# Retention's rotary halves crossed by ScalarE while it evacuates a block, and top-k rounds moved behind the rotations

## The chip, the cores and the metric

The kernel runs on one core of one Trainium2 chip. The metric is the device time of one execution in microseconds (us); the time before is the median of 3 runs. Engines are called PE (TensorE, the matmuls), DVE (VectorE), ACT (ScalarE), POOL (GpSimd) and SP (SyncE, which issues DMAs).

## The reference

One inference step of a two-layer decoder trunk for 256 prompt tokens and 8 x 8 sample tokens, 320 tokens in all. What matters here is the first layer's mixer (`even_mixer`), in fp32:

```python
proj = h @ p['w_in_even'][e]
q, k, v, qi, wi, ki, rq, rk, rv, rg = jnp.split(proj, points, axis=-1)
...
rq = rope(rq.reshape(B, L, RET_HEADS, RET_HEAD_DIM), pos, inv_r)
rk = rope(rk.reshape(B, L, RET_HEADS, RET_HEAD_DIM) * (RET_HEAD_DIM ** -0.5), pos, inv_r)
...
def rope(x, pos, inv_freq):      # half = 64 of a head's 128 for retention, 8 of 64 for the attention
    x1, x2 = xf[..., :half], xf[..., half:rot]
    return concat([x1 * cos - x2 * sin, x2 * cos + x1 * sin, xf[..., rot:]])
```

The other head group picks keys by `lax.top_k` of an indexer's score (64 of 256 prompt keys, 66 of 264 keys for the samples).

## The kernel before

Every engine has its own instruction stream, written out by hand; semaphores order them. Features lie on the 128 partitions, the 320 tokens along a row. The input projection of the mixer (stage `even_in`) gives 26 blocks of 128 output features. A block is 8 contraction chunks of 3 matmuls (`three_passes`, lines 1610 to 1612: the weight's high part times the activation's high and low part, and the weight's low part times the high one), each 128x320. Two blocks share a weight tile (`w_raw`, 1 MB, two slots). Before PE may use a tile, ACT rounds it to `w_hi` (line 1880, two instructions) and DVE subtracts to get `w_lo` (line 2073, two instructions); SP loads the tile after next into `w_raw` once `w_lo` is done. ACT evacuates a finished block from one of four PSUM banks to `proj` (line 857) and signals `p_evac`.

Blocks 0 to 7 hold the attention's and indexer's queries and keys, 10 to 17 the retention's queries and keys (`B_RQK` = 10), 18 to 25 its values and gates. Blocks 0 to 7 and 10 to 17 are rotated in place:

```python
pe.matmul(ps[:, 4 + r % 2, 0:TOK], perm[:, kind, :], proj[:, b, :], ...)            # L589, the halves swapped and signed
dve.tensor_tensor(rope_a[:, par, :], src, ropet[:, 2 * kind, :], ALU.mult)          # L965, times cos
steps.did(dve.tensor_tensor(rope_b[:, par, :], ps[:, 4 + par, 0:TOK], ...))         # L967, times sin, waits rope_mm
dve.tensor_tensor(src, rope_a[:, par, :], rope_b[:, par, :], ALU.add)               # L970
```

The program names `rope_a` and `rope_b` as `f`, whose memory they use. PE issues the permutation product of block b-1 behind all of block b's matmuls, and small products of the indexer behind some blocks (`after(b)`). DVE goes round once for every two blocks b, b+1 (`dve_even`): `w_lo` of the next tile, then the two rotations, then what the step has besides: index scores, and rounds of the top-k (`top`: MAX of 8, MATCH_REPLACE; lines 975 and 977), which overwrite the 8 largest scores of each row; `mask` (lines 983 and 985) turns what was taken into a bias. `scores[0]` is 128 wide (first 128 queries), `scores[1]` 256, `score_s` 326. All of this must be done before the attention, which begins with `logits(0)` on PE, a MEMSET (line 1142) and `soft(0)` on DVE, after the last block's evacuation. The rest of `score_s`'s rounds stand in the attention. In the attention PE multiplies with the retention state `st_in` (line 735), which POOL loads after the last evacuation, and streams weights of the conditioning (line 1675).

Of the kernel before, what the change touches and what calls it, by code (L numbers as in the profile page):

```python
# [23 lines left out]
P = 128  # L24
# [3 lines left out]
ALU = mybir.AluOpType  # L28
# [9 lines left out]
TOK = PTOK + STOK  # L38
# [14 lines left out]
HD = 64  # L53
# [19 lines left out]
B_RQK = 10  # L73
# [73 lines left out]
CR = 2  # L147
# [41 lines left out]
def build(nc, t):  # L189

    with ExitStack() as ctx:
        sems = {}

        def sem(name):
            if name not in sems:
                sems[name] = ctx.enter_context(nc.semaphore(name))
            return sems[name]
# [65 lines left out]
        ps = ctx.enter_context(nc.psum_tensor("ps", [P, 8, 512], F32))  # L263
# [15 lines left out]
        stack, pb = phase()  # L279
# [6 lines left out]
        stack, pb = phase()  # L286
# [4 lines left out]
        stack.close()  # L291
        stack, pb = phase()
        proj = pb("proj", [P, EVEN_BLOCKS, TOK])
        perm = pb("perm", [P, 2, P])
        cached = pb("cached", [P, NB, 3, PAST])

        bias_p = pb("bias_p", [P, 2, PTOK])
# [154 lines left out]


        p_evac = sem("p_evac")
        rope_mm = sem("rope_mm")
        rope_done = sem("rope_done")
        perm_in, rope_in = sem("perm_in"), sem("rope_in")
        even_in_dma, even_const = sem("even_in_dma"), sem("even_const")
# [104 lines left out]
        def even_constants(sp_):  # L563

            sp_.wait_ge(w_used, CR + W_BASE["even_in"])
            sp_.wait_ge(moments_done, SUB["down0"] + 1)
            sp_.dma_start(perm[:, :, :], t["perm"]).then_inc(perm_in, 16)
# [14 lines left out]
        def pe_even(pe, three_passes, w_half, two_tiles, ada_pieces, ada_transpose):  # L582
            base = W_BASE["even_in"]

            def rotate(b, r, kind):

                pe.wait_ge(p_evac, PB + b + 1)
                pe.wait_ge(rope_done, CR + r - 1)
                pe.matmul(ps[:, 4 + r % 2, 0:TOK], perm[:, kind, :], proj[:, b, :], start=True, stop=True)\  # L589
                  .then_inc(rope_mm, 1)  # L590

            def block_of(n, b, bank, slot_, h):
# [77 lines left out]

            two_tiles("even_in", True)
            pe.wait_ge(row_ready, 6)
            rotate(0, 0, 0)
            rotate(1, 1, 0)
            for b in range(4, EVEN_BLOCKS):
                block_of(base + b // 2, b, b % 4, (base + b // 2) % 2, b % 2)
                if b <= 9:
                    rotate(b - 2, b - 2, 0)
                elif B_RQK < b <= B_RQK + 8:
                    rotate(b - 1, b - 1 - (B_RQK - 8), 1)  # L680
                after(b)


# [161 lines left out]
        def act_even(act, steps, split_w, n_half, ada_copy):  # L845
            base = W_BASE["even_in"]

            def evacuate(t_, j, b, kinds):

                if t_:  # L850
                    split_w(base + t_ + 1, (base + j + 1) % 2)
                for h in range(2):
                    if h == 0:
                        act.wait_ge(half_used, t_ + 1)
                    else:
                        act.wait_ge(w_used, CR + base + t_ + 1)
                    act.activation(proj[:, b + h, :], ps[:, 2 * j + h, 0:TOK], kinds[h][0], scale=kinds[h][1])\
                       .then_inc(p_evac, 1)

# [98 lines left out]
        def dve_even(dve, steps, split_w, softplus, ada_bias):  # L958
            base = W_BASE["even_in"]

            def rotate(b, r, par, kind):

                dve.wait_ge(p_evac, PB + b + 1)
                src = proj[:, b, :]
                dve.tensor_tensor(rope_a[:, par, :], src, ropet[:, 2 * kind, :], ALU.mult)  # L965
                dve.wait_ge(rope_mm, r + 1)
                steps.did(dve.tensor_tensor(rope_b[:, par, :], ps[:, 4 + par, 0:TOK], ropet[:, 2 * kind + 1, :],  # L967
                                            ALU.mult))
                steps.wait()
# [33 lines left out]
            for b in range(0, EVEN_BLOCKS, 2):  # L1003
# [28 lines left out]
                    dve.reduce_sum(wis1[:, :], wis[:, :, :], axis=AX).then_inc(wis_ready, 1)  # L1032
                    score(0, 0, range(NIH))
                if B_RQK <= b < B_RQK + 8:
                    rotate(b, b - B_RQK + 8, 0, 1)
                    rotate(b + 1, b - B_RQK + 9, 1, 1)
                if b == 12:
                    top(scores[0], 3)
                elif b == 14:
                    score(1, 1, (0, 1))  # L1040
                    score(1, 2, (2, 3))
                    top(scores[0], 2)
                elif b == 16:
                    top(scores[0], 3)
                    mask(scores[0], bias_p[:, 0, 0:P])
                elif b == 18:
                    dve.wait_ge(wis_ready, 1)
                    for bh in range(2):
                        dve.wait_ge(relu_ready, 4 + bh)
                        last = dve.tensor_scalar(relu[:, 1 - bh, 0:KEYS_S], relu[:, 1 - bh, 0:KEYS_S],  # L1050
                                                 wis1[:, bh:bh + 1], None, ALU.mult)
                    last.then_inc(weighed, 1)
                    top(scores[1], 3)
                elif b == 20:
                    top(scores[1], 3)
                elif b == 22:
                    top(scores[1], 2)
                    mask(scores[1], bias_p[:, 1, :])
                    dve.wait_ge(ixs_done, 1)
                    steps.did(dve.tensor_tensor(score_s[:, 0:KEYS_S], ps[0:STOK, 6, 0:KEYS_S], bias_s[:, :], ALU.add))  # L1060
                    steps.wait()
                    top(score_s[:, :], 2)
                elif b == 24:
                    top(score_s[:, :], 1)

            def spread(h):
                dve.wait_ge(tr_v, h + 1)
# [1381 lines left out]
def tables():  # L2449
# [7 lines left out]
    perm = np.zeros((P, 2, P))  # L2457
# [4 lines left out]
    for kind, starts, half, inv in ((0, (0, HD), 8, inv_a), (1, (0,), 64, inv_r)):  # L2462
        ang = pos[None, :] * inv.astype(np.float32)[:, None]
        for s in starts:
            for i in range(half):
                perm[s + half + i, kind, s + i] = -1.0
                perm[s + i, kind, s + half + i] = 1.0
            for o in (s, s + half):
                rope[o:o + half, 2 * kind] = np.cos(ang)
                rope[o:o + half, 2 * kind + 1] = np.sin(ang)  # L2470
    out["perm"], out["rope"] = perm, rope

    lg = np.array(LN_G)
# [124 lines left out]
```

## Time and profile before

| | us |
|---|---|
| median of 3 runs | 1431.97 (1431.39, 1431.97, 1434.85) |
| profiled execution, own time | 1434.27 |
| its span | 1431.4 |
| PE busy | 1362.2 |
| DVE busy | 790.0 |
| ACT busy | 613.5 |

Times within the trace count from the span's start. `even_in` runs from about 320 to 428 us; block 10 begins at about 355 us, block 12 at 366.04, block 18 at 396.07, block 22 at 413.71, and the last matmul of block 25 starts at 427.74. The attention follows until about 504 us. Matmuls overlap in the trace: one is shown longer than the distance to the next.

### The profile page before, as it was taken

Reading aid. Unit: us, or ns where it says so; the run is one execution under the profiler, and the core shown is the slowest. Engines: PE = TensorE matmul, PEld = TensorE weight load, DVE = VectorE, ACT = ScalarE, POOL = GpSimd, SP = SyncE. Lnnn points to the kernel's source line nnn. Section 1 sums busy time; section 2 is a strip of 40 time slices with the busy share of each in tenths; the row PEclk is TensorE's granted clock in tenths of the full one; section 3 lists DMA queues with packets and bytes.
Section 4 is the critical chain, followed back from the end, with each engine's and each line's share of the span. In section 5 each row is a group of like instructions: output and inputs, shape, how many; then the busy total and the mean of one; then the engine's idle time right before and its main releaser. Section 6 shows DMA issues by size and latency. Waiting matters only on the chain.

```text
span 1431.4 us, 24385 instructions
## 1 busy us (share of the span) xinstructions
PE 1362.2 (95%) x9798; PEld 1258.6 (88%) x9798; DVE 790.0 (55%) x1446; ACT 613.5 (43%) x1043; POOL 87.6 (6%) x139
## 2 busy tenths in 40 slices
PE   5899999999998998999999899999989999999996
PEld 1799999989885697999999799999978888999996
DVE  1543444566686877444455644444567976444444
ACT  2433333444342365333344533344358755443332
POOL 0000000003001101000000100000010110000000
PEclk7799999999999999999999999999999999999998
DMA  9466655466248665564444555544466653444342
GB/s 362 184 206 205 201 180 183 153 207 225 89 150 289 257 237 203 178 206 160 135 140 155 208 188 195 175 129 142 152 257 222 200 178 114 147 147 147 125 153 83
DMA packets 82259, 260.07 MB, mean 182 GB/s; under 512 B 11634, under 2 KB 22962, under 8 KB 82034
## 3 DMA queue, kind: packets, MB, share of 16 engines
q1 hardware_dynamic: 65682, 199.56, 41.6%
q0 software_dynamic: 16480, 59.15, 11.7%
q8 instruction: 68, 1.11, 0.3%
q14 instruction: 29, 0.24, 0.1%
HBM read 254.45 MB, written 4.23 MB: 181 GB/s over the span
## 4 chain that ended last, share of the span: by engine, by line
PE 82%; DVE 11%; ACT 3%; DMA 2%; issue 2%; SPq 0%; DVEq 0%; ACTq 0%
PE ps L1610 25%; PE ps L1612 24%; PE ps L1611 24%; PE ps L1675 3%; DVE w_lo L2073 2%; DVE f L2155 1%; DVE x L2141 1%; DVE f L2161 1%; DVE f L2137 1%; DMA a_raw<-in_ada 1%; DMA x<-in_x 1%; DVE xn_lo L2149 1%; DMA st_in<-in_state_ret 1%; PE ps L1697 1%; ACT xn_hi L1938 1%
## 5 line engine op out<-in xcount | busy, mean ns | idle before, releaser
L1610 PE MATMUL ps<-xn_hi,w_hi 128*128 128x320 f32 x1808 | 573.8, 317 | 24.8 <-DVE xn_lo L2149 19.2
L1612 PE MATMUL ps<-xn_hi,w_lo 128*128 128x320 f32 x1808 | 561.1, 310 | 0.0
L1611 PE MATMUL ps<-xn_lo,w_hi 128*128 128x320 f32 x1808 | 560.8, 310 | 0.0
L2073 DVE TENSOR_TENSOR w_lo<-w_raw,w_hi 128x1024 fp32r<-128x1024 f32 (+1 forms) x357 | 382.4, 1109 | 125.1 <-ACT w_hi L1880 124.6
L1610 PEld LDWEIGHTS ps<-xn_hi,w_hi 128*128 128x128 f32 x1808 | 341.6, 189 | 55.0 <-issue 29.6
L1880 ACT ACTIVATE w_hi<-w_raw 128x1024 fp32r<-128x1024 f32 x362 | 331.6, 961 | 86.0 <-PE ps L1612 78.7
L1611 PEld LDWEIGHTS ps<-xn_lo,w_hi 128*128 128x128 f32 x1808 | 341.8, 189 | 1.3
L1612 PEld LDWEIGHTS ps<-xn_hi,w_lo 128*128 128x128 f32 x1808 | 341.5, 189 | 0.0
L1610 PE MATMUL ps<-mid_hi,w_hi 128*128 128x320 f32 x704 | 218.3, 310 | 0.3 <-DVE w_lo L2073 0.3
L1612 PE MATMUL ps<-mid_hi,w_lo 128*128 128x320 f32 x704 | 217.3, 309 | 0.0
L1611 PE MATMUL ps<-mid_lo,w_hi 128*128 128x320 f32 x704 | 217.3, 309 | 0.0
L2237 DVE TENSOR_TENSOR hbuf<-ps,sil 128x320 f32<-128x320 f32 x88 | 43.2, 491 | 239.5 <-ACT sil L1958 239.5
L1958 ACT ACTIVATE sil<-ps 128x320 f32<-128x320 f32 x88 | 38.4, 436 | 316.3 <-PE ps L1612 316.3
L1610 PEld LDWEIGHTS ps<-mid_hi,w_hi 128*128 128x128 f32 x704 | 132.2, 188 | 2.3 <-issue 1.6
L1611 PEld LDWEIGHTS ps<-mid_lo,w_hi 128*128 128x128 f32 x704 | 132.2, 188 | 0.0
L1612 PEld LDWEIGHTS ps<-mid_hi,w_lo 128*128 128x128 f32 x704 | 132.2, 188 | 0.0
L1675 PE MATMUL ps<-a_raw,c 128*32 128x256 f32 x896 | 72.3, 421 | 18.2 <-DMA a_raw<-in_ada 17.9
L535 POOL DMA_DIRECT2D a_raw<-in_ada x96 | 51.1, 534 | 528.9 <-PE ps L1675 512.7
L2242 DVE TENSOR_TENSOR mid_lo<-hbuf,mid_hi 128x320 fp32r<-128x320 f32 (+1 forms) x88 | 43.3, 493 | 49.7 <-ACT mid_hi L1962 49.7
L1962 ACT ACTIVATE mid_hi<-hbuf 128x320 fp32r<-128x320 f32 (+1 forms) x88 | 41.5, 472 | 53.4 <-DVE hbuf L2237 53.4
L1971 ACT ACTIVATE sq<-ps 128x320 f32<-128x320 f32 x43 | 18.7, 436 | 102.2 <-PE ps L1612 102.2
L1675 PEld LDWEIGHTS ps<-a_raw,c 128*32 128x32 f32 x896 | 21.4, 113 | 45.8 <-DMA a_raw<-in_ada 22.8
(282 smaller groups left out, 967.2 us busy)
## 6 DMA issues: line engine op xcount, KB each, us to landing
w_raw<-in_gu SPq DMA_DIRECT2D x176, 512.0 KB, 4.6
a_raw<-in_ada POOLq DMA_DIRECT2D x96, 512.0 KB, 4.9
w_raw<-in_down SPq DMA_DIRECT2D x64, 512.0 KB, 3.6
w_raw<-in_pj SPq DMA_DIRECT2D x58, 512.0 KB, 4.8
w_raw<-in_down SPq DMA_DIRECT2D x64, 192.0 KB, 3.6
a_raw<-in_ada SPq DMA_DIRECT2D x16, 512.0 KB, 7.8
w_raw<-in_ada SPq DMA_DIRECT2D x16, 512.0 KB, 7.1
lent_hi<-in_ada SPq DMA_DIRECT2D x8, 512.0 KB, 9.8
```

The source lines that it names most:

```text
L535: gp.dma_start(a_raw[:, r % A_SLOTS, :], row(t["ada"], p)).then_inc(a_landed[r % A_SLOTS], 16)
L1610: pe.matmul(out, hi, xhi, start=start, stop=False)
L1611: pe.matmul(out, hi, xlo, start=False, stop=False)
L1612: return pe.matmul(out, w_lo[s][:, w_at:w_at + P], xhi, start=False, stop=stop)
L1675: last = pe.matmul(ps[32 * g:32 * (g + 1), out, cols], c32[:, k, :], part[:, ADA_COLS * g:ADA_COLS * (g + 1)], start=(k == 0), stop=(k == ...
L1880: act.activation(w_hi[s][:, cols], w_raw[:, s, cols], ACT.Copy).then_inc(w_high, 1)
L1958: act.activation(sil[:, j, :], ps[:, 2 * j, 0:TOK], ACT.Silu).then_inc(sil_ready, 1)
L1962: act.activation(at(mid_hi, 2 * i + j), hbuf[:, j, :], ACT.Copy).then_inc(mid_high, 1)
L1971: act.activation(sqacc[:, :] if first else sq2[:, b, :], ps[:, bank, 0:TOK], ACT.Square).then_inc(sq_ready, 1)
L2073: dve.tensor_tensor(w_lo[s][:, cols], w_raw[:, s, cols], w_hi[s][:, cols].bitcast(F32), ALU.subtract).then_inc(w_split, 1)
L2237: dve.tensor_tensor(hbuf[:, j, :], ps[:, 2 * j + 1, 0:TOK], sil[:, j, :], ALU.mult)\
L2242: dve.tensor_tensor(at(mid_lo, 2 * i + j), hbuf[:, j, :], at(mid_hi, 2 * i + j).bitcast(F32), ALU.subtract).then_inc(mid_ready, 1)
```

## The change

For blocks 10 to 17 the permutation product goes. In its place ACT, when it evacuates such a block, first reads PSUM twice more, 64 partitions each, and writes the upper half of the features into the lower half of `rope_b` and the other way round; then it does the evacuation as before. It waits until the rotation two blocks ago has freed that half of `rope_b`, and signals `crossed`. DVE multiplies `rope_b` by the sines (whose sign for the first half now lies in the table), `proj` by the cosines in place, and adds. `perm` shrinks from 2 x 128 to 128 columns. The rotations of blocks 0 to 7 stay as they are. The top-k rounds are given out differently over the steps of DVE; their number is the same.

```diff
@@ pe_even @@
                 if b <= 9:
-                    rotate(b - 2, b - 2, 0)
-                elif B_RQK < b <= B_RQK + 8:
-                    rotate(b - 1, b - 1 - (B_RQK - 8), 1)
+                    rotate(b - 2, b - 2)
                 after(b)
@@ act_even, evacuate @@
+                    if B_RQK <= b < B_RQK + 8:
+                        act.wait_ge(rope_done, CR + b + h - 3)
+                        for to, of in ((0, HD), (HD, 0)):
+                            last = act.activation(rope_b[to:to + HD, h, :], ps[of:of + HD, 2 * j + h, 0:TOK], kinds[h][0],
+                                                  scale=kinds[h][1])
+                        last.then_inc(crossed, 1)
                     act.activation(proj[:, b + h, :], ps[:, 2 * j + h, 0:TOK], kinds[h][0], scale=kinds[h][1])\
@@ dve_even @@
+            def rotate_halves(b, par):
+
+                dve.wait_ge(p_evac, PB + b + 1)
+                src = proj[:, b, :]
+                dve.wait_ge(crossed, b - B_RQK + 1)
+                steps.did(dve.tensor_tensor(rope_b[:, par, :], rope_b[:, par, :], ropet[:, 3, :], ALU.mult))
+                steps.did(dve.tensor_tensor(src, src, ropet[:, 2, :], ALU.mult))
+                steps.wait()
+                dve.tensor_tensor(src, src, rope_b[:, par, :], ALU.add).then_inc(rope_done, 1)
...
-                    rotate(b, b - B_RQK + 8, 0, 1)
-                    rotate(b + 1, b - B_RQK + 9, 1, 1)
+                    rotate_halves(b, 0)
+                    rotate_halves(b + 1, 1)
                 if b == 12:
-                    top(scores[0], 3)
+                    top(scores[0], 1)
```

Rounds per step of DVE (step b stands behind the rotations of b and b+1), written as score x rounds:

| step | before | after |
|---|---|---|
| 12 | scores[0] x3 | scores[0] x1 |
| 14 | scores[0] x2 | scores[0] x1 |
| 16 | scores[0] x3, mask | scores[0] x1 |
| 18 | scores[1] x3 | scores[0] x4 |
| 20 | scores[1] x3 | scores[0] x1, mask, scores[1] x3 |
| 22 | scores[1] x2, mask, score_s x2 | scores[1] x3, score_s x1 |
| 24 | score_s x1 | scores[1] x2, mask, score_s x2 |

On DVE the step of blocks 12 and 13, from its first rotation to its last round, stood before as

```order
L965 TENSOR_TENSOR f<-proj,f 128x320 [waits p_evac,relu_used]
L967 TENSOR_TENSOR f<-ps,f 128x320 [waits rope_mm]
L970 TENSOR_TENSOR proj<-f 128x320 [waits dve_step]
L965 TENSOR_TENSOR f<-proj,f 128x320 [waits p_evac]
L967 TENSOR_TENSOR f<-ps,f 128x320 [waits rope_mm]
L970 TENSOR_TENSOR proj<-f 128x320 [waits dve_step]
L975 MAX top<-score_p 128x8
L977 MATCH_REPLACE score_p<-top,score_p 128x128 [waits dve_step]
L975 MAX top<-score_p 128x8 [waits dve_step]
L977 MATCH_REPLACE score_p<-top,score_p 128x128 [waits dve_step]
L975 MAX top<-score_p 128x8 [waits dve_step]
L977 MATCH_REPLACE score_p<-top,score_p 128x128 [waits dve_step]
```

and stands now, the next tile's `w_lo` included, as

```order
L970 TENSOR_TENSOR f<-f 128x320 [waits crossed,p_evac,relu_used]
L971 TENSOR_TENSOR proj<-proj,f 128x320
L973 TENSOR_TENSOR proj<-proj,f 128x320 [waits dve_step]
L970 TENSOR_TENSOR f<-f 128x320 [waits crossed,p_evac]
L971 TENSOR_TENSOR proj<-proj,f 128x320
L973 TENSOR_TENSOR proj<-proj,f 128x320 [waits dve_step]
L989 MAX top<-score_p 128x8
L991 MATCH_REPLACE score_p<-top,score_p 128x128 [waits dve_step]
L2089 TENSOR_TENSOR w_lo<-w_raw,w_hi 128x1024 [waits w_high,dve_step]
```

The product's PSUM result (`f<-ps`, waiting for `rope_mm`) is gone from the rotation, which now waits for `crossed` at its first instruction, and two of the three rounds are gone from in front of `w_lo`.

On ACT the evacuations of blocks 12 and 13, the two `relu` evacuations of the indexer and the next tile's `w_hi` stood before as

```order
L857 ACTIVATE proj<-ps 128x320 [waits half_used]
L857 ACTIVATE proj<-ps 128x320 [waits w_used]
L955 ACTIVATE relu<-ps 128x512 [waits ix_done]
L955 ACTIVATE relu<-ps 128x512 [waits relu_used,ix_done]
L1880 ACTIVATE w_hi<-w_raw 128x1024 [waits w_landed00,w_used]
L1880 ACTIVATE w_hi<-w_raw 128x1024 [waits w_landed01]
```

and stand now as

```order
L858 ACTIVATE f<-ps 64x320 [waits rope_done,half_used]
L858 ACTIVATE f<-ps 64x320
L861 ACTIVATE proj<-ps 128x320
L858 ACTIVATE f<-ps 64x320 [waits rope_done,w_used]
L858 ACTIVATE f<-ps 64x320
L861 ACTIVATE proj<-ps 128x320
L959 ACTIVATE relu<-ps 128x512 [waits ix_done]
L959 ACTIVATE relu<-ps 128x512 [waits relu_used,ix_done]
L1896 ACTIVATE w_hi<-w_raw 128x1024 [waits w_landed00,w_used]
L1896 ACTIVATE w_hi<-w_raw 128x1024 [waits w_landed01]
```

Each evacuation has two 64-partition instructions ahead of it, and the next tile's `w_hi` comes behind them.

On DVE the last step of the stage, from `w_lo` of the following stage's tile to the attention's first instruction (MEMSET of `qz`), stood before as

```order
L2073 TENSOR_TENSOR w_lo<-w_raw,w_hi 128x1024 [waits w_high,dve_step]
L2073 TENSOR_TENSOR w_lo<-w_raw,w_hi 128x1024 [waits w_high]
L975 MAX top<-score_s 64x8
L977 MATCH_REPLACE score_s<-top,score_s 64x326 [waits dve_step]
L1142 MEMSET qz 128x576 [waits rope_done,p_evac,dve_step]
```

and stands now, from the second of the two `w_lo` instructions on, as

```order
L2089 TENSOR_TENSOR w_lo<-w_raw,w_hi 128x1024 [waits w_high]
L989 MAX top<-score_p 128x8
L991 MATCH_REPLACE score_p<-top,score_p 128x256 [waits dve_step]
L989 MAX top<-score_p 128x8 [waits dve_step]
L991 MATCH_REPLACE score_p<-top,score_p 128x256 [waits dve_step]
L997 TENSOR_SCALAR score_p<-score_p 128x256 [waits dve_step]
L999 TENSOR_TENSOR bias_p<-bias_p,score_p 128x256 [waits dve_step]
L989 MAX top<-score_s 64x8
L991 MATCH_REPLACE score_s<-top,score_s 64x326 [waits dve_step]
L989 MAX top<-score_s 64x8 [waits dve_step]
L991 MATCH_REPLACE score_s<-top,score_s 64x326 [waits dve_step]
L1158 MEMSET qz 128x576 [waits rope_done,p_evac,dve_step]
```

Four rounds and a mask stand now where one round stood.

## Rows read from the trace of the kernel before

**Rows 1.** Windows, blocks 12 to 25: us; busy (count) PE, PEld, DVE, ACT, POOL; clock, DMA.
```profile
363.37:428.05 64.68, 62.23 (x410) 55.77 (x408) 47.97 (x112) 23.88 (x38) 0.00 (x0) 1.00 0.37 124
```

**Rows 2.** Waits of 326 to 436: who waited for whom, us, times, longest.
```profile
DVE f L967 <- PE ps L589: 20.1, 10, 4.9
PE ps L1610 <- DVE w_lo L2073: 2.1, 3, 1.3
```

**Rows 3.** Timeline of PE: start, us, instruction, [idle before].
```profile
342.68 0.55 PE L1610 MATMUL ps<-xn_hi,w_hi 128*128 128x320 f32 x1
...
346.74 0.55 PE L1610 MATMUL ps<-xn_hi,w_hi 128*128 128x320 f32 x1
...
385.98 0.41 PE L1610 MATMUL ps<-xn_hi,w_hi 128*128 128x320 f32 x1 [0.35 <-DVE w_lo L2073]
...
396.07 0.41 PE L1610 MATMUL ps<-xn_hi,w_hi 128*128 128x320 f32 x1 [0.45 <-DVE w_lo L2073]
...
405.25 0.42 PE L1610 MATMUL ps<-xn_hi,w_hi 128*128 128x320 f32 x1 [1.34 <-DVE w_lo L2073]
...
414.25 0.30 PE L1610 MATMUL ps<-xn_hi,w_hi 128*128 128x320 f32 x1
...
417.77 0.31 PE L1610 MATMUL ps<-xn_hi,w_hi 128*128 128x320 f32 x1
```

**Rows 4.** Instructions of line 589: min/median/max ns.
```profile
L589 PE MATMUL ps<-proj,perm x32: 430/431/432, 329.7 to 400.0; 128*128 128x320 f32 x32
```

**Rows 5.** Timeline of DVE.
```profile
370.40 0.49 DVE L967 TENSOR_TENSOR f<-ps,f 128x320 f32<-128x320 f32 x1 [4.88 <-PE ps L589]
...
391.80 1.53 DVE L992 SCALAR_TENSOR_TENSOR score_p<-relu,wi_tok,score_p 128x256 f32<-128x256 f32 x3
...
418.27 0.43 DVE L975 MAX8 top<-score_p 128x8 f32<-128x256 f32 x1
...
419.26 0.30 DVE L983 TENSOR_SCALAR score_p<-score_p 128x256 f32<-128x256 f32 x1
...
419.93 0.47 DVE L1060 TENSOR_TENSOR score_s<-ps,bias_s 64x320 f32<-64x320 f32 x1
...
421.55 0.49 DVE L975 MAX8 top<-score_s 64x8 f32<-64x326 f32 x1
...
422.67 2.36 DVE L2073 TENSOR_TENSOR w_lo<-w_raw,w_hi 128x1024 fp32r<-128x1024 f32 x2
...
428.76 0.54 DVE L1142 MEMSET qz<- 128x576 f32 x1 [2.75 <-issue]
```

**Rows 6.** Timeline of ACT.
```profile
364.28 0.28 ACT L874 ACTIVATE vtok<-ps 64x128 f32<-64x128 f32 x1
...
395.17 0.98 ACT L955 ACTIVATE relu<-ps 128x320 f32<-128x320 f32 x2 [0.86 <-PE ps L630]
...
421.05 0.44 ACT L857 ACTIVATE proj<-ps 128x320 f32<-128x320 f32 x1 [3.08 <-PE ps L1612]
421.38 2.00 ACT L1880 ACTIVATE w_hi<-w_raw 128x1024 fp32r<-128x1024 f32 x2
```

**Rows 7.** The page, part 6: KB each, us to landing.
```profile
w_raw<-in_pj SPq DMA_DIRECT2D x58, 512.0 KB, 4.8
```

**Rows 8.** Timeline of PE in the attention.
```profile
432.29 0.71 PE L714 MATMUL ps<-vt,kt 128*128 128x128 f32 x4 [0.22 <-DVE am_s L1079]
...
437.57 2.00 PE L735 MATMUL ps<-qz,st_in 128*128 128x64 f32 x16 [2.16 <-DMA st_in<-in_state_ret]
...
439.90 3.52 PE L1675 MATMUL ps<-w_raw,c 128*32 128x256 f32 x32
...
473.57 1.93 PE L1675 MATMUL ps<-w_raw,c 128*32 128x256 f32 x32
```

**Rows 9.** Windows in the attention, columns as in Rows 1.
```profile
440.00:444.00 4.00, 4.00 (x48) 1.91 (x52) 0.00 (x0) 0.77 (x2) 2.39 (x3) 0.60 0.47 143
456.00:460.00 4.00, 2.71 (x28) 1.33 (x32) 3.85 (x7) 0.60 (x2) 2.35 (x3) 0.60 0.36 94
```

More of the change, by code:

```diff
@@ L293, in build @@
         proj = pb("proj", [P, EVEN_BLOCKS, TOK])
-        perm = pb("perm", [P, 2, P])
+        perm = pb("perm", [P, P])
         cached = pb("cached", [P, NB, 3, PAST])
@@ L454, in build @@
         p_evac = sem("p_evac")
-        rope_mm = sem("rope_mm")
+        rope_mm, crossed = sem("rope_mm"), sem("crossed")
         rope_done = sem("rope_done")
@@ L566, in even_constants @@
             sp_.wait_ge(moments_done, SUB["down0"] + 1)
-            sp_.dma_start(perm[:, :, :], t["perm"]).then_inc(perm_in, 16)
+            sp_.dma_start(perm[:, :], t["perm"]).then_inc(perm_in, 16)
             sp_.dma_start(ones_h[:, :], t["ones_h"]).then_inc(perm_in, 16)
@@ L583, in pe_even, with rotate @@
             base = W_BASE["even_in"]
-            def rotate(b, r, kind):
+            def rotate(b, r):
                 pe.wait_ge(p_evac, PB + b + 1)
                 pe.wait_ge(rope_done, CR + r - 1)
-                pe.matmul(ps[:, 4 + r % 2, 0:TOK], perm[:, kind, :], proj[:, b, :], start=True, stop=True)\
+                pe.matmul(ps[:, 4 + r % 2, 0:TOK], perm[:, :], proj[:, b, :], start=True, stop=True)\
                   .then_inc(rope_mm, 1)
@@ L672, in pe_even @@
             pe.wait_ge(row_ready, 6)
-            rotate(0, 0, 0)
-            rotate(1, 1, 0)
+            rotate(0, 0)
+            rotate(1, 1)
             for b in range(4, EVEN_BLOCKS):
@@ L1041, in dve_even @@
                     score(1, 2, (2, 3))
-                    top(scores[0], 2)
+                    top(scores[0], 1)
                 elif b == 16:
-                    top(scores[0], 3)
-                    mask(scores[0], bias_p[:, 0, 0:P])
+                    top(scores[0], 1)
                 elif b == 18:
@@ L1052, in dve_even @@
                     last.then_inc(weighed, 1)
-                    top(scores[1], 3)
+                    top(scores[0], 4)
                 elif b == 20:
+                    top(scores[0], 1)
+                    mask(scores[0], bias_p[:, 0, 0:P])
                     top(scores[1], 3)
                 elif b == 22:
-                    top(scores[1], 2)
-                    mask(scores[1], bias_p[:, 1, :])
+                    top(scores[1], 3)
                     dve.wait_ge(ixs_done, 1)
@@ L1061, in dve_even @@
                     steps.wait()
+                    top(score_s[:, :], 1)
+                elif b == 24:
+                    top(scores[1], 2)
+                    mask(scores[1], bias_p[:, 1, :])
                     top(score_s[:, :], 2)
-                elif b == 24:
-                    top(score_s[:, :], 1)
             def spread(h):
@@ L2455, in tables @@
            "sel4": np.kron(np.eye(4), np.eye(32, NCOND))}
-    perm = np.zeros((P, 2, P))
+    perm = np.zeros((P, P))
     rope = np.zeros((P, 4, TOK))
@@ L2465, in tables @@
             for i in range(half):
-                perm[s + half + i, kind, s + i] = -1.0
-                perm[s + i, kind, s + half + i] = 1.0
+                if kind == 0:
+                    perm[s + half + i, s + i], perm[s + i, s + half + i] = -1.0, 1.0
             for o in (s, s + half):
                 rope[o:o + half, 2 * kind] = np.cos(ang)
-                rope[o:o + half, 2 * kind + 1] = np.sin(ang)
+                rope[o:o + half, 2 * kind + 1] = np.sin(ang) * (-1.0 if kind and o == s else 1.0)
     out["perm"], out["rope"] = perm, rope
```

## The prediction, made before the changed kernel was run

> **What bounds the kernel now.** I read the page first: PE is busy for 1362.2 of 1431.4 us, so time comes off only where PE works or waits. Then the windows of the changed stretch: from the product behind block 11 to the end of block 25 PE is busy for 62.23 of 64.68 us, DVE for 47.97, ACT for 23.88, at a granted clock of 1.00 [rows 1]. The stage is PE's, but DVE is at 74%, and the waits show where it matters: PE waits three times for `w_lo`, 2.1 us in all, while DVE waits 20.1 us in ten rotations for the permutation product [rows 2]. The timeline of PE names the places: 0.35 us before block 16, 0.45 before block 18, 1.34 before block 20, together 2.14 [rows 3]. So DVE is late with the next tile although it has stood idle before, because the product of block b stands behind all matmuls of block b+1: 4.88 us of waiting in one rotation [rows 5].
>
> **Removed: eight products on PE.** With a product between them, two block starts lie 346.74 - 342.68 = 4.06 us apart. Without one, eight groups of three matmuls (a whole block) take 417.77 - 414.25 = 3.52 us [rows 3]. A product costs 0.54 us, and eight 4.3 us. Nothing else keeps PE there: it is busy throughout, so the whole of it comes off, if DVE delivers the tiles that much earlier.
> The records themselves would say more: two of 431 ns for each product [rows 4], 8 x 0.862 = 6.9 us. The Trainium skill (Trainium Kernel Development and Optimization, Performance Expectations) says that matmul busy time misleads because matmuls are pipelined; by starts one gets 4.3, by durations 6.9. The distance of starts is a measurement of this stage, so I take 4.3; 6.9 is a rival.
>
> **Removed: the rotation's wait.** DVE's instructions stay three per rotation, 128x320 each; one that read PSUM took 0.49 us [rows 5], and no row suggests that reading SBUF instead costs more. So a rotation is at most 1.5 us as before. What goes is the wait for the product.
>
> **Added: 16 evacuations of 64 partitions on ACT.** No row has this form. Nearest below: 64x128 from PSUM, 0.28 us; nearest above: 128x320, 0.44 us [rows 6]. The form has the same 320 columns as the latter, so I take 0.44, which started one after another lie 0.33 apart (421.38 - 421.05) [rows 6]. All of it is 16 x 0.28 to 0.44 = 4.5 to 7.0 us on an engine that is idle for 40.8 of 64.68 us [rows 1], so its price is only lateness: an evacuation is signalled about 0.7 us later, and the next tile's `w_hi` (2.00 us for two [rows 6]) follows that much later. That is 0.35 from the last matmul's start to ACT, 1.1 for three evacuations, 2.0 for `w_hi`, then half of 2.36 for the last half of `w_lo` [rows 5]: 4.7 us of the 7.05 that PE spends on a tile. Covered; without that cover it would cost 0.7 us a tile, 2.8 in four.
> The new wait on ACT (the rotation two blocks ago) holds the evacuation and whatever stands behind it, `w_hi` and PE's bank. That rotation is a full tile old; with DVE at the times below it is done 3 us or more earlier. Nothing.
>
> **Moved: the rounds. Is DVE in time?** Two tiles decide it. Tile 18 (blocks 18, 19) must be half ready when PE gets there: 396.07 less 0.80 of waits and seven products is 391.5. On DVE stand before it the rotation of block 15, four score instructions and one round. Block 15's matmuls end at 385.98 - 0.35 - 5 x 0.54 = 382.9; evacuated by 384.4; rotated by 385.9; scores at 0.51 each [rows 5] by 388.0; a round, at most the 0.99 of one twice as wide (419.26 - 418.27 [rows 5]), by 389.0; first half of `w_lo` by 390.2. That is 1.3 us in hand. Tile 20: needed at 405.25 - 2.14 - 4.32 = 398.8. Block 17 ends about 390.1, evacuated 391.5, two `relu` (0.98 [rows 6]) behind the index products by 392.5, `w_hi` first half 393.5; the rotation and one round are over at 394.0; `w_lo` both halves by 396.4, 2.4 in hand. Before, three rounds and a mask stood there. With two rounds more (2.0 us) it would still hold, so most of what relieves PE is the vanished wait, not the new distribution. All three waits go: 2.14 us.
> Steps 18 to 22 hold `w_lo` 2.36, at most four rounds at 0.99 and up to 0.7 besides, 7.0 us of DVE against a tile of 7.05; with the time in hand they hold. The weights: ACT's `w_hi` waits for no load in this stage, and a load lands 4.8 us after issue [rows 7], with a tile of 7.05 between; nothing.
>
> **Given back? The last step.** After block 23's evacuation (421.05 in the old times) `w_hi`'s first half is ready at about 422.4. DVE then has `w_lo` 2.36, two rounds of `scores[1]` at 0.99, the mask 0.67 (419.93 - 419.26) and two rounds of `score_s` at 1.12 (422.67 - 421.55) [rows 5]: 4.9 us, so it ends at 429.6. The MEMSET that opens the attention started at 428.76 after 2.75 us of idleness [rows 5]. So DVE comes 0.85 us late, and behind the MEMSET are queued the first logits, the copies of values and the decay products, for which PE already waited 0.22 us. But PE then waits 2.16 us for the state `st_in` [rows 8], whose load hangs on the last evacuation and not on the rounds. The 0.85 us comes out of this wait. Nothing, until the delay passes 2.1 us.
>
> **Sum.** 4.3 + 2.1 = 6.4 us. On the profiled execution's own time 1434.27 gives 1427.9. That execution lay 2.3 above the median of the runs; on the median, 1431.97 - 6.4 = 1425.5 us.
>
> **The rivals.**
> *Products only (15%).* The waits for `w_lo` stay, because DVE or ACT is later than I reckon (above all at tile 18, with 1.3 us in hand). For it: DVE's step 14 holds up to 2.36 + 3.0 + 2.04 + 0.99 = 8.4 us of work against a tile of 7.05. Against: the ends worked out above. 1431.97 - 4.3 = 1427.7; half the waits, 1426.6.
> *Full length of the records (8%).* 6.9 + 2.1 = 9.0 us, 1423.0. Against it is the distance of block starts.
> *The gain is lost in the attention (15%).* PE arrives 6.4 us earlier, but `st_in` or the lent weights land no earlier: DMA, not PE, sets that stretch. For it: PE's 2.16 us wait there ended on a DMA. Against: that load is issued by the last evacuation and moves with it. 1430 to 1432.
> *The clock.* After waits the granted clock fell to 0.60 on average over 440 to 444 and over 456 to 460 [rows 9]; 32 matmuls of line 1675 then took 3.52 us against 1.93 at full clock [rows 8], 1.6 us for one such dip. Moving the waits can add or spare one: 1427.1 or 1423.9. I give this 25% inside the forecast, as width. The Trainium skill (TensorE: Matmul & The Clock Gate, What's actually happening) says that an idle PE is throttled and activity releases it, and that the monitor does not restart with a kernel; by that the same kernel can show one dip more or less from run to run, which the spread of the three runs (1431.39 to 1434.85) would allow.
> *Slower (4%).* The last step overruns: PE then waits for DVE at the attention's start. Price: overrun less the 2.1 us that the wait for `st_in` covers. It eats the gain at an overrun of 8.5 us, ten times what I reckon; at 13 us the kernel takes 1436.4. For it: four rounds and a mask stand where one round stood, and a second engine, ACT, waits for the same logits. Against: the price of each round is in the rows.
>
> **How the numbers follow.** A change within 0.3% (4.3 us) is what a measurement of this kernel cannot tell from none. The forecast has 58%: 1423.9 to 1427.3 with the clock's width. With the full records (8%) and half of "products only" it makes 0.73, of which I take 0.02 off for an added dip: faster 0.71. The other half, the lost gain and most of those 0.02 make same 0.24; slower 0.05. The range takes 1421.5 (full records and a spared dip) to 1430.0 (products only and a dip more, or most of the gain lost); outside lie the rest of the lost gain and slower.
>
> **What would show it.** In the profile after: no line 589 matmul beyond block 7; block starts 3.5 us apart from block 13 on where no small product stands between; no PE wait for `w_lo` between blocks 12 and 25; 64x320 evacuations of about 0.44 us; no rotation of blocks 10 to 17 that waits for PE; the MEMSET of `qz` about 0.8 us later behind the last evacuation, and the wait for `st_in` that much shorter; the last block's end near 421.5 instead of 428. The prediction is wrong if a wait for `w_lo` or for an evacuation reappears on PE, if the crossing evacuations take over 1 us, or if the wait before line 735 grows by what the stage gained.

## The result, and the profile after the change

| | median, us | lowest to highest | runs |
|---|---|---|---|
| before | 1433.49 | 1431.39 to 1434.85 | 5 |
| changed | 1425.45 | 1422.27 to 1427.18 | 5 |

The ratio is 0.994, with a 95% interval of 0.9923 to 0.9956: 8.0 us faster by the medians, 6.3 to 11.0 by the interval. The forecast was 6.4 us and 1425.5. Its starting point was the median of three runs, 1431.97, which with two runs more became 1433.49; so the time fits better than the gain does. Medians here and below leave out two executions that ran far slower at a lower granted clock (1512.94 us at 0.843, 1733.42 us at 0.723). The profiled execution took 1425.45 us, its span 1423.8 against 1431.4.

I read the gain between two events that both kernels have: the last rotation that uses a product (block 7), and the attention's first logits on PE. The windows of before, then of the changed kernel (us; busy and count of PE, PEld, DVE, ACT, POOL; clock; DMA share, GB/s); the first line of each is that stage, the second the attention up to the first matmul of the output projection:

```profile
355.31:428.58 73.27, 70.29 (x463) 63.34 (x461) 55.38 (x144) 26.58 (x43) 0.00 (x0) 1.00 0.33 113
428.58:507.68 79.10, 71.45 (x733) 46.41 (x733) 54.85 (x131) 29.52 (x85) 14.01 (x21) 0.96 0.76 275
```

```profile
354.55:420.80 66.25, 65.40 (x446) 60.75 (x444) 54.46 (x142) 33.27 (x59) 0.00 (x0) 1.00 0.38 125
420.80:499.98 79.18, 71.72 (x732) 46.77 (x733) 55.73 (x134) 29.65 (x85) 14.00 (x21) 0.96 0.76 274
```

The stage is 7.02 us shorter and the attention 0.08 longer. It began 0.76 us earlier already (355.31, 354.55), in front of anything that the change touches; that part is not the change's: in the fourteen profiled executions of this document the stage begins anywhere from 354.30 to 356.83. Behind, everything stands 7.7 us earlier.

The waits of the changed kernel in the stage (who waited for whom: us in all, times, longest); the one PE row is the last wait, for block 25's evacuation, and none is for `w_lo` as in [rows 2]:

```profile
DVE f L970 <- ACT proj L861: 5.3, 4, 2.1
DVE w_lo L2089 <- ACT w_hi L1896: 3.7, 5, 1.6
...
PE ps L750 <- ACT proj L861: 0.5, 1, 0.5
```

DVE after: block 15's rotation, `w_lo` of tile 18 and of tile 20, and the MEMSET that opens the attention. They answer to [rows 5].

```profile
383.61 0.49 DVE L970 TENSOR_TENSOR f<-f 128x320 f32<-128x320 f32 x1 [2.10 <-ACT proj L861]
...
387.75 2.36 DVE L2089 TENSOR_TENSOR w_lo<-w_raw,w_hi 128x1024 fp32r<-128x1024 f32 x2
...
393.40 2.36 DVE L2089 TENSOR_TENSOR w_lo<-w_raw,w_hi 128x1024 fp32r<-128x1024 f32 x2
...
422.05 0.54 DVE L1158 MEMSET qz<- 128x576 f32 x1 [0.19 <-DVE score_s L991]
```

ACT after: block 17's crossing, and the stage's last evacuation ([rows 6]).

```profile
389.28 0.87 ACT L858 ACTIVATE f<-ps 64x320 f32<-64x320 f32 x2 [2.18 <-PE ps L1628]
390.18 0.44 ACT L861 ACTIVATE proj<-ps 128x320 f32<-128x320 f32 x1
...
420.31 0.44 ACT L861 ACTIVATE proj<-ps 128x320 f32<-128x320 f32 x1 [3.08 <-PE ps L1628]
```

PE after: block 18's start, then the attention ([rows 3, 8]).

```profile
390.44 0.42 PE L1626 MATMUL ps<-xn_hi,w_hi 128*128 128x320 f32 x1
...
420.80 0.49 PE L750 MATMUL ps<-proj 64*128 64x128 f32 x4 [0.53 <-ACT proj L861]
...
424.87 0.71 PE L712 MATMUL ps<-vt,kt 128*128 128x128 f32 x4 [0.57 <-DVE am_s L1095]
...
429.61 2.00 PE L733 MATMUL ps<-qz,st_in 128*128 128x64 f32 x16 [1.62 <-DMA st_in<-in_state_ret]
...
431.90 3.33 PE L1691 MATMUL ps<-w_raw,c 128*32 128x256 f32 x32
...
449.39 3.57 PE L1691 MATMUL ps<-w_raw,c 128*32 128x256 f32 x32 [1.49 <-DVE f L1147]
...
487.98 1.93 PE L1691 MATMUL ps<-w_raw,c 128*32 128x256 f32 x32 [1.99 <-DVE proj L1101]
```

The reader is to see that block 18 starts without a bracket, so PE found its tile ready, and that the MEMSET's idleness of 2.75 us in [rows 5] has shrunk to 0.19: DVE now runs through the stage's end. What that costs PE is moved, not added: 0.22 has become 0.57 at the decay product, 2.16 has become 1.62 at the state.

### The profile page after: what moved, and what is told of

It is laid out like the page before. It is cut to its first block, busy times and chain, and to the rows that moved or that the text cites. A ratio compares the mean times of both kernels' runs of the same rounds, so it can differ in the third digit from the quotient of the medians.

```text
span 1423.8 us, 24378 instructions
## 1 busy us (share of the span) xinstructions
PE 1357.0 (95%) x9782; PEld 1255.8 (88%) x9782; DVE 789.6 (55%) x1446; ACT 620.6 (44%) x1059; POOL 87.5 (6%) x139
## 4 chain that ended last, share of the span: by engine, by line
PE 83%; DVE 9%; ACT 3%; DMA 2%; issue 2%; SPq 0%; DVEq 0%; ACTq 0%
PE ps L1626 26%; PE ps L1628 25%; PE ps L1627 25%; PE ps L1691 3%; DVE f L2171 1%; DVE w_lo L2089 1%; DVE x L2157 1%; DVE f L2177 1%; DVE f L2153 1%; DVE xn_lo L2165 1%; DMA x<-in_x 1%; DMA a_raw<-in_ada 1%; DMA st_in<-in_state_ret 1%; PE ps L1256 1%; PE ps L1713 1%
```

## The experiments

Twelve kernels, four each on three chips; each four were timed beside the kernel before on the same chip (medians 1433.40, 1434.28 and 1434.08 there). The changed kernel itself was not timed beside them. "Stage" and "attention" are the two windows above, in the kernel's profiled execution, with the attention's granted clock.

| kernel | median, us (runs) | ratio (95%) | stage | attention | clock |
|---|---|---|---|---|---|
| old_rounds | 1425.94 (6) | 0.9942 (0.9925 to 0.9958) | 66.23 | 83.50 | 0.90 |
| new_rounds_only | 1433.48 (12) | 0.9999 (0.9988 to 1.0009) | 70.55 | 82.29 | 0.92 |
| product_kept | 1431.90 (11) | 0.9991 (0.9980 to 1.0001) | 70.55 | 77.66 | 0.96 |
| cross_twice | 1426.07 (8) | 0.9949 (0.9930 to 0.9969) | 66.25 | 79.07 | 0.96 |
| late_old_rounds | 1440.33 (7) | 1.0043 (1.0026 to 1.0060) | 78.76 | 81.00 | 0.94 |
| late_new_rounds | 1431.06 (10) | 0.9981 (0.9968 to 0.9993) | 71.64 | 76.34 | 1.00 |
| heavy_tail | 1425.72 (4) | 0.9944 (0.9922 to 0.9966) | 66.25 | 78.72 | 0.98 |
| state_first | 1426.69 (6) | 0.9948 (0.9930 to 0.9965) | 66.23 | 79.11 | 0.94 |
| rounds_behind | 1424.68 (6) | 0.9938 (0.9924 to 0.9952) | 66.22 | 76.30 | 0.98 |
| behind_state_first | 1422.84 (5) | 0.9925 (0.9909 to 0.9940) | 66.25 | 75.49 | 0.98 |
| plus_variance | 1421.23 (6) | 0.9912 (0.9896 to 0.9928) | 66.25 | 73.26 | 1.00 |
| half_products | 1430.04 (12) | 0.9964 (0.9948 to 0.9981) | 68.39 | 80.43 | 0.94 |

**Old rounds.** The changed kernel with the distribution of before.

```diff
                 if b == 12:
-                    top(scores[0], 1)
+                    top(scores[0], 3)
...
```

> The crossing by ScalarE with the top-k rounds given out as in the kernel before. Measure: the stretch from block 7's last product-bound rotation instruction on DVE (line 967 of before) to the attention's first logits on PE, 73.3 us in before and 66.25 in the changed kernel. My theory (the rotation's wait for a product behind the next block is what made DVE late): no wait for w_lo returns, the stretch stays at 66.3 +-0.3 and the time within 1 us of the changed kernel. Rival (the new distribution of the rounds removes the waits): the waits of 0.35, 0.45 and 1.34 us before blocks 16, 18 and 20 come back, the stretch is about 69 us.

The stage took 66.23 us, as in the changed kernel, and PE waited in it only the 0.5 at its end. The new distribution gives nothing in this stage once the product is gone. (The profiled execution, with its attention of 83.50 us, was the slowest of the six.)

**New rounds only.** The kernel before with the new distribution.

> The kernel before with the new distribution of the rounds alone, products kept. If each half of the change by itself is enough for the waits (the rounds in front of w_lo shrink by 1.4, 0.7 and 1.9 us at tiles 16, 18 and 20, more than the waits of 0.35, 0.45 and 1.34): the stretch falls from 73.3 to 70.6 us, all of it from the waits. If only the vanished wait for the product helps: it stays above 72.5. In either case DVE ends its last step 1 to 1.5 us behind the last evacuation, and the wait for the state on PE shrinks by that.

The stage took 70.55 us, 2.72 less than before, and no `w_lo` wait was left. So with the products in place the distribution does take the waits away, and they were worth more than the 2.14 us in their brackets. The median did not move, though. In the profiled execution the attention was 3.2 us longer than before's; that this holds for the other eleven is not shown. PE's timeline there:

```profile
453.68 3.64 PE L1677 MATMUL ps<-w_raw,c 128*32 128x256 f32 x32 [1.75 <-DVE f L1133]
...
493.50 3.53 PE L1677 MATMUL ps<-w_raw,c 128*32 128x256 f32 x32 [2.00 <-DVE proj L1087]
```

Two such groups, each 1.6 to 1.7 us over the 1.93 of full speed, stand behind a wait. The granted clock was 0.50 and 0.52 over them, the lower of the two levels (1.2 GHz).

**The product kept.** The changed kernel with eight products more, which read `x`, wait for the evacuation as before's did, and whose result nobody uses.

```diff
+                elif B_RQK < b <= B_RQK + 8:
+                    pe.wait_ge(p_evac, PB + b)
+                    pe.matmul(ps[:, 4 + (b - 1) % 2, 0:TOK], perm[:, :], x[:, b % KC, :], start=True, stop=True)
```

> The changed kernel with eight 128x320 products put back on PE at their old places; they read another fp32 tile, and nobody uses the result (work is added, the output is unchanged). A product costs what the distance of starts says: 0.54 us each, the stretch grows from 66.25 to 70.6 us, with no wait for w_lo. Rival (the length of the records): 0.86 us each, 73.1 us. Rival (part of it is hidden): under 69 us.

Its products by form (min/median/max ns, first and last start), and its windows:

```profile
L681 PE MATMUL ps<-x,perm x16: 430/430/431, 362.9 to 398.4; 128*128 128x320 f32 x16
```

```profile
354.83:425.38 70.55, 69.70 (x463) 63.42 (x461) 54.55 (x142) 33.48 (x59) 0.00 (x0) 1.00 0.35 118
425.38:503.04 77.66, 70.55 (x733) 46.87 (x733) 55.74 (x134) 29.65 (x85) 14.04 (x21) 0.96 0.78 279
```

70.55 - 66.25 = 4.30 us for eight products: 0.54 each, although their records say 2 x 0.430. The rival "full length of the records" falls.

**Half of the products.** Four of them, behind blocks 11, 13, 15 and 17.

> The changed kernel with four unused products put back (blocks 10, 12, 14, 16) instead of eight: does the whole time follow the stretch? The stretch should be 66.25 + 4 x 0.54 = 68.4 us. If the time follows it, about 1428 us and 2.2 above the changed kernel run beside it. Rival (the time outside the stretch depends on where in it the clock falls after waits): 1.5 us or more away from that on either side, with the difference in the attention.

The stage took 68.39, halfway to 0.01 us. The median stood higher than the stage says: 1430.04, where 1427.6 would have been, so the rival's 1.5 us is met. Three of twelve runs took 1424.3 to 1424.7, at a mean granted clock of 0.989, the others 1429.2 to 1434.1 at 0.978 to 0.984. The profiled execution (1429.71) belongs to the latter and has an attention of 80.43 at a clock of 0.94: of its 4.26 us over the changed kernel's profiled execution 2.14 are in the stage, 1.25 in the attention and 0.75 in front of both.

**Crossing twice.** ACT does the two 64-partition evacuations again into the free `rope_a`, 16 more in all.

```diff
+                        for to, of in ((0, HD), (HD, 0)):
+                            act.activation(rope_a[to:to + HD, h, :], ps[of:of + HD, 2 * j + h, 0:TOK], kinds[h][0],
+                                           scale=kinds[h][1])
```

> The changed kernel with each crossing done twice, the second into the unused half of the rotary scratch: 16 more evacuations of 64 partitions, about 0.9 us later per block for everything behind them on ACT, 7 us more work on ACT in all. My theory (ACT's part is hidden; tile 18 has over 1 us in hand): the stretch stays within 0.3 us of 66.25. Rival (ACT is close to being the bound): each of the four tiles is 0.9 us later, the stretch grows to about 69 to 70 us.

Stage 66.25, and no wait on PE but the one for block 25's evacuation. Another 0.9 us per evacuation is still covered, so that ACT's new work costs nothing here is shown, with a margin as large as the work.

**Late rotation, with the old and with the new rounds.** The rotation waits for the next block's evacuation; nothing else changes. That is later than the product's result had come: block 11's rotation ended 3.0 us after the start of block 12's last matmul here, and 1.8 us after it in the kernel before.

```diff
-                dve.wait_ge(p_evac, PB + b + 1)
+                dve.wait_ge(p_evac, PB + b + 2)
```

> The changed kernel with the rounds of before, and with each rotation of blocks 10 to 17 held until the next block is evacuated too: the lateness of the product is back, the product is not. If the lateness together with the old rounds made the waits for w_lo, they return: 2.5 to 3.2 us on the stretch (66.25 to about 69), at blocks 16, 18 and 20. Rival (the products' own load on PE pushed DVE out of step): the stretch stays at 66.3.

> The same late rotations with the new rounds. By the last run of the rounds alone (70.55, no wait for w_lo) the new rounds suffice: the stretch is 66.3 to 66.8 us. Rival (the products gave DVE the time that this needed, a tile is now 7.05 and not 8.1 us): a wait for w_lo of 1 us or more returns at block 18 or 20, 67.5 or more.

Both expectations missed. With the old rounds the waits did return before blocks 16, 18 and 20, but the stage grew by 12.5 us and not by 2.5 to 3.2; with the new rounds it grew by 5.4, as the rival had it. PE's timeline with the old rounds, then with the new:

```profile
376.10 2.25 PE L617 MATMUL ps<-proj 64*128 64x256 f32 x8 [1.18 <-DVE wis L1046]
...
388.23 0.41 PE L1624 MATMUL ps<-xn_hi,w_hi 128*128 128x320 f32 x1 [2.65 <-DVE w_lo L2087]
...
399.55 0.42 PE L1624 MATMUL ps<-xn_hi,w_hi 128*128 128x320 f32 x1 [2.76 <-DVE w_lo L2087]
...
410.60 0.41 PE L1624 MATMUL ps<-xn_hi,w_hi 128*128 128x320 f32 x1 [2.22 <-DVE w_lo L2087]
```

```profile
374.36 2.25 PE L617 MATMUL ps<-proj 64*128 64x256 f32 x8 [1.18 <-DVE wis L1046]
...
385.06 0.41 PE L1626 MATMUL ps<-xn_hi,w_hi 128*128 128x320 f32 x1 [1.22 <-DVE w_lo L2089]
...
395.66 0.41 PE L1626 MATMUL ps<-xn_hi,w_hi 128*128 128x320 f32 x1 [2.04 <-DVE w_lo L2089]
...
403.28 0.41 PE L1626 MATMUL ps<-xn_hi,w_hi 128*128 128x320 f32 x1 [0.31 <-DVE w_lo L2089]
```

With the products gone PE has only 7.05 us for a tile, and a rotation that comes late pushes `w_lo` out of it: 8.8 us of waits with the old rounds (7.6 for `w_lo`, 1.2 for `wis`), of which the new rounds take 4.1 away. Most of the other 3.7 of the 12.5 us is clock. Behind the waits of 2.76 and 2.22 us, but not behind the one of 2.65, PE ran 1.4 and 0.5 us at full pace and then 14 intervals between matmuls were about 0.27 us each in place of 0.147. The window over the first such stretch, with a granted clock of 0.50:

```profile
401.10:404.40 3.30, 3.30 (x14) 3.30 (x13) 0.83 (x2) 0.00 (x0) 0.00 (x0) 0.50 0.81 258
```

So the early rotation carries the change (66.23 against 78.76 with the old rounds, 66.25 against 71.64 with the new). That the new rounds alone would not have carried it is shown only for a rotation 1.2 us later than the product's; at the product's own pace it was not run. The wait of 2.04 us at block 18 is more than those 1.2, so by my estimate some of it would have been left.

**Heavy tail.** Three rounds of `scores[1]` moved from step 22 to step 24, 3.0 us more in front of the MEMSET.

> The changed kernel with three 256-wide rounds moved from the step of block 22 to the last step: DVE ends its last step about 3.0 us later, with nothing else moved. My reading of the attention's start (the delay comes out of the wait for the retention state, 1.62 us left) says: the MEMSET lies 4.7 us behind the last evacuation instead of 1.74, the wait for the state vanishes, and about 1.4 us more or less of the delay reaches the later attention. Rival (the rounds' place is free, other waits take all of it): the first conditioning matmul is no later behind the first logits than the 11.1 us of the changed kernel. Rival (no cover at all): it is 3.0 us later.

The MEMSET started 4.68 us behind the last evacuation's start instead of 1.74. PE waited 2.62 and 0.83 us for DVE, and no longer for the state. The first conditioning matmul stood 13.96 us behind the first logits (11.10 in the changed kernel), twice the delay expected: PE's waits up to there grew by 1.3 us, about as expected, and the rest came from the clock (0.53 over 428 to 431). And yet the attention was no longer than the changed kernel's (78.72, 79.18), for its first two groups both ran at full clock, 1.93 us each in place of 3.33 and 3.57. The second:

```profile
450.32 1.93 PE L1690 MATMUL ps<-w_raw,c 128*32 128x256 f32 x32 [1.49 <-DVE f L1146]
```

**The state first.** SP holds four weight loads back until the state has landed.

```diff
+                        sp_.wait_ge(st_landed, 16)
```

> The changed kernel, with four of the conditioning's weight loads (512 KB each, on SP's queue) held until the first retention state has landed: the load that PE waits 1.62 us for then has the DMA engines to itself. Theory (the state is late because it shares them): it lands in 4 to 6 us instead of 8.7, the wait of 1.62 us goes, the first conditioning matmul comes 1.0 to 1.6 us earlier behind the first logits (11.1 to about 9.8 us), and the kernel gains 1 to 1.6 us. Rival (the load's own latency rules, not the company): it lands as late as before, and the held loads may then be late for their own matmuls: no gain or a loss of up to 2 us.

The first state landed 4.9 us after its issue instead of 8.5 and its wait went, but PE then waited as long for DVE:

```profile
432.80 2.73 PE L1692 MATMUL ps<-w_raw,c 128*32 128x256 f32 x32 [1.50 <-DVE f L1147]
```

The first conditioning matmul came 10.98 us behind the logits instead of 11.10, and the median was no better (1426.69): the expected gain of 1 to 1.6 us did not come. So DVE stands right behind the load in that place, and the 2.1 us by which I said the last step is covered is no slack of DVE's.

**Taking those waits away.** Three kernels build on this. In the attention the rounds of `score_s` go behind `divide(2h+1)`; then the state first as well; then also the last variance ahead of `soft(N_PU + 1)`.

```diff
                 soft(2 * h + 1)
-                if h < 2:
-                    top(score_s[:, :], score_rounds // 3)
-                elif h == 2:
+                if h == 2:
                     mask(score_s[:, :], bias_s[:, :])
...
                 divide(2 * h + 1)
+                if h < 2:
+                    top(score_s[:, :], score_rounds // 3)
...
-            soft(N_PU + 1)
             variance(RH - 1)
+            soft(N_PU + 1)
```

> The changed kernel, with the three rounds of score_s in each of the attention's first two heads moved from in front of the state update and the copy that PE waits for to behind the head's last division, where DVE stands idle for 5.8 and 3.8 us. Theory (those 3.3 us of DVE are what the conditioning matmuls of the second head wait for): the wait of 1.49 us on DVE before them goes; the first head keeps its 1.62 us wait for the state; gain 1.5 us at one clock. Rival (the wait moves to the next step of DVE): no gain.

> The same, with the four weight loads also held until the first state has landed. With the rounds out of the way the earlier state can be used: the first conditioning matmul comes 9.5 us behind the first logits instead of 11.1; 3.1 us off in all. Rival (the held loads are now late for their own matmuls, which would start at 32 matmuls or 1.9 us further): a wait for them of 1 to 2 us appears and eats the 1.6.

> The same again, with the last head's variance on DVE put ahead of the last logits' evacuation. PE's wait of 1.99 us for it falls by about 1.5; 4.5 us off the changed kernel in all if nothing takes the waits' place, about 1421. Rival (the logits' chain becomes the last thing): under 0.5 us more than the kernel without this edit.

In the first of them the wait of 1.49 us is gone, and the median is 0.8 us under the changed kernel's where 1.5 was expected. In the second the first conditioning matmul comes 9.42 us behind the logits (9.5 expected); of the rival's wait for the held loads 0.68 us appears. In the third the wait of 1.99 us falls by 1.4, and 1421.23 stands where about 1421 was expected.

The last of them in the attention, its window and the conditioning groups whose long waits went:

```profile
423.08:496.34 73.26, 68.81 (x732) 45.37 (x733) 55.58 (x134) 29.76 (x85) 13.99 (x21) 1.00 0.83 297
```

```profile
448.04 1.93 PE L1692 MATMUL ps<-w_raw,c 128*32 128x256 f32 x32 [0.45 <-DVE f L1147]
...
483.83 1.93 PE L1692 MATMUL ps<-w_raw,c 128*32 128x256 f32 x32 [0.58 <-DVE proj L1101]
```

The waits of 1.49 and 1.99 us are down to 0.45 and 0.58, all four groups run at 1.93 and the clock is 1.00 throughout. Its 1421.23 us is 0.9912 of before beside it, the fastest version here; it beats the kernel before by 12.9 us and stands 4.2 below the changed kernel's 1425.45, though those two were not timed together. Its attention is 5.9 us shorter than the changed kernel's. Part of that is clock: late_new_rounds has the changed kernel's instructions there and the same long waits, and in its profiled execution they ran at a clock of 1.00 in 76.34 us. By that, 2.8 of the 5.9 us are clock and 3.1 are waits. Its window, and its group behind the wait of 1.49 us:

```profile
426.60:502.94 76.34, 68.52 (x732) 45.55 (x733) 56.15 (x135) 29.66 (x85) 14.03 (x21) 1.00 0.80 286
```

```profile
453.93 1.93 PE L1691 MATMUL ps<-w_raw,c 128*32 128x256 f32 x32 [1.49 <-DVE f L1147]
```

## Why the prediction was right, and where a size was off

*The number.* The median came out at 1425.45 us for 1425.5 forecast. That it fits to 0.05 us is luck: the starting point lay 1.5 us under the median of five runs, and the sum 0.6 us under what the stage gave. From 1433.49 the same sum gives 1427.1.

*Eight products, 4.3 us.* Right: 4.30 by the product kept, 2.14 by half of them. Neither ACT nor DVE took any of it back.

*The three waits, 2.14 us.* The mechanism was right, the size was not: the term "Moved: the rounds", "All three waits go: 2.14 us", measured 2.72 (new rounds only; and 7.02 - 4.30 for the changed kernel). I had added up the brackets. A bracket counts from the modelled end of the last matmul, 0.31 us long, while the next one could have started 0.147 behind it; and the first matmul after the pause holds PE longer. Before, around block 20 (the wait itself is in [rows 3]):

```profile
403.61 0.31 PE L1612 MATMUL ps<-xn_hi,w_lo 128*128 128x320 f32 x1
...
405.50 0.31 PE L1611 MATMUL ps<-xn_lo,w_hi 128*128 128x320 f32 x1
```

From 403.61 to 405.25 are 1.64 us in place of 0.147, from 405.25 to 405.50 0.25 in place of 0.147: 1.6 us for a bracket of 1.34. The sum should have read 4.3 + 2.7 = 7.0, by which the median would have been forecast at 1425.0. It is the error that I had avoided with the products, where I went by starts: there the records said too much (0.86 us for 0.54 of time), here they said too little. The Trainium skill (Trainium Kernel Development and Optimization, Performance Expectations) says that matmul busy time is a bad measure of how close a kernel is to its roofline, because matmuls are pipelined. The trace agrees in so far as 0.86 us of records stand for 0.54 of time.

*"Most of what relieves PE is the vanished wait, not the new distribution."* Right for the changed kernel: the old rounds give 66.23 without it. But the other versions show more than I had said. With products, the distribution alone removes the waits; without, the early rotation alone does, and the distribution alone does not when the rotation comes 1.2 us later than the product's. The 20.1 us of waiting in ten rotations with which I argued are those of the whole of [rows 2]; about 12.7 us in five rotations belong to blocks 10 to 17, the rest to rotations that stay as they were.

*Tiles 18 and 20.* The first half of tile 18's `w_lo` was ready at 388.9, block 18 started at 390.44: 1.5 us in hand, 1.3 forecast. Tile 20 was whole at 395.7, PE there about 397.5: 1.8 in hand, 2.4 forecast.

*Crossing evacuations.* The size of one was right (0.43 us, taken 0.44), their distance was not: I took 0.33, a pair took 0.90 from its first start to the next evacuation's, so the delay per block is 0.90 us, not 0.7. Covered, as crossing twice shows.

*The last step.* DVE came 1.07 us later by the MEMSET (behind the last evacuation's start 0.67 before, 1.74 now), 0.85 forecast. As forecast it came out of the wait for the state: the first conditioning matmul stood 11.32 us behind the logits before, 11.10 now.

*The rivals.* "Products only" falls, with no `w_lo` wait left. "The gain is lost in the attention" did not happen to this change (79.10, 79.18) but did to new_rounds_only in its profiled execution, at a lower clock (0.92) and not through DMA: its wait for the state was 1.54 us against 2.16 before. "Slower by an overrun" was priced as if PE's first delay decided; 3 us of overrun moved the first conditioning matmul by 2.86 us, and the median hardly (1425.72).

*The clock.* As width it was priced at one slowed group, 1.6 us; the forecast's upper end of 1427.3 should read 1427.1 by that price. In the profiled pair no such group more or less is found: two were slowed before (3.52, 3.37 us) and two after (3.33, 3.57). Elsewhere it makes much of the difference between attentions. In the profiled executions the attention took from 73.3 to 83.5 us, at a clock of 1.00 down to 0.90, while the stage's clock stayed at 1.00 but for late_old_rounds. Where the clock falls is not fixed by the wait ahead: the changed kernel ran a group at 1.93 behind a wait of 1.99, new rounds only one at 3.53 behind 2.00. Over the fourteen profiled executions the conditioning group in third place, which has no wait in front, took 1.93 us every time. The one in second place was slowed in 8 of the 11 executions with a wait of 1.49 to 1.75 us in front, and in none of the 3 where that wait was gone or 0.45 us; the one in fourth place in 4 of the 13 with a wait of 1.99 or 2.00, and not in plus_variance behind 0.58. So waits and slowed groups go together here, and not each time; what decides is not shown. The Trainium skill (TensorE: Matmul & The Clock Gate, What's actually happening) says that throttling is the default state and activity releases it. By that, waits among the attention's few matmuls invite it; plus_variance, with small waits and a clock of 1.00, agrees. late_new_rounds, with the long waits and a clock of 1.00 all the same, shows that they do not enforce it.

*Open.* The stage's gains and those of the whole time do not match one by one. new_rounds_only has a stage 2.7 us shorter than before and the same median; the medians of product_kept (1431.90) and half_products (1430.04) lie 2.2 and 2.4 us above the changed kernel's 1425.45 plus 4.3 or 2.14. So by medians the products seem to be worth more than 4.3 us and the waits less than 2.7. Why is not shown: one execution of each has a profile, and the changed kernel was not timed beside them (its own interval is 4.7 us wide, though four kernels with its stage and nearly its attention, from old_rounds to state_first, have medians of 1425.7 to 1426.7). For half_products the stage, the clock and the later start account for its profiled execution. For product_kept the clock gives no account: its runs at the highest clocks, 0.993 and 0.991, took 1430.89 and 1431.44, and its profiled execution, with a short attention, took 1429.38, the least of all. A part lies outside the spans: in the three kernels with eight products behind blocks 11 to 18 the time exceeds the span by 1.6 to 3.3 us from run to run, in the eleven others by 1.6 to 1.7 in every run. That is 0.7 us of product_kept's 2.2, and 1.2 of the 8.8 us between the profiled executions of before and after; its cause is open.

## What to carry to other kernels

Count a stall of PE from start to start of its matmuls, at the pace that it would have kept, and not by the idle time in brackets; the same holds for what a matmul costs. When work is taken off PE, the tile that the other engines have to meet becomes shorter by as much, so a reordering that was enough before may be too little after, and must be priced against the new tile. Small waits among sparse matmuls can be worth more than their length, since in this kernel the conditioning group behind a wait of 1.5 to 2.0 us ran at low clock in 12 of 24 cases, and the later three groups never did where the wait was gone or short.

## What the runs showed of the hardware that I had not expected

- Two evacuations of 64 partitions x 320 from PSUM, whose halves change place, took 0.43 us each and did not overlap: 0.90 from the first start to the next instruction's. A 128x320 evacuation was followed by the next instruction after 0.33 to 0.34. Half the partitions save nothing.
- The first load of the state landed in 4.9 us instead of 8.5 when four weight loads waited for it.
- 32 conditioning matmuls took 1.93 us at full clock and up to 3.64 where it was low (0.50 over that group), and which groups were hit changed from one execution to the next.
- The clock also fell in the stage, where PE is dense: to 0.50 for over 3 us behind single waits of 2.76 and 2.22 us (late_old_rounds), and not behind one of 2.65.
